# First operand from a channel-major copy of x; token-major x, its norm and the bias table later

## The chip, the cores and the metric

The kernel runs on one core of one Trainium2 chip. A core has TensorE (matmuls), VectorE, ScalarE, GpSimd and SyncE (which here only issues DMAs); the five run side by side, each takes its own instructions in order, and they wait for each other through semaphores. Sixteen DMA engines carry the loads of all queues. The metric is the device time of one execution in microseconds; the number that counts is the median of several.

## The reference, cut to what matters

Two transformer blocks run over 256 tokens of 2048 channels. All weights are read once, some 570 MB. The change is in the first step of the first block:

```
h    = x * rsqrt(mean(x*x) + eps) * g_mix_pre          # norm over the channels
proj = h @ w_in                                        # 2048 -> 5920
q, k, v ... = split(proj)                              # four kinds of attention, with bias tables
x    = x + rmsnorm(mix, g_mix_post)                    # x is needed again, token-major
```

The norm's factor is one number per token, so proj is (x * g_mix_pre) @ w_in, times that factor.

## The kernel before

**Operands.** A float32 product is made of three fp32r products: both operands are split into a top (rounded) and a rest, and top x top, rest x top and top x rest are summed in PSUM. ScalarE rounds a weight (`hi`, L769, writes w_hi), VectorE subtracts (`lo`, L1354, writes w_lo). The first operand lies with channels on partitions, in 16 chunks of 128 channels: HH (top) and HL (rest), tile h_hi_lo.

**Blocks and units.** The product goes block by block, 512 output columns each; blocks 0 to 11 are w_in. A block has 8 units, a unit two chunks of channels: 24 matmuls of 128 x 256 in block 0 (L2344; unit 0 of block 0 has lines of its own, L2329 and L2335). Weights come by SyncE's DMAs in tiles w_raw of 1 MB, four to a block, each for two units; a tile is loaded again once `lo` has read it (`weight_tile`, L471). ScalarE and VectorE run four units ahead of TensorE: in slot s they do the weights of unit s + 4 (`slot`, SPLIT_LEAD), each instruction in the order of the code.

**x at the start.** Only the token-major x is loaded, in pieces between the first weight tiles. `turn_first(j)` on TensorE transposes two chunks (four 128 x 128 transposes, L2519) into a PSUM bank, ScalarE multiplies by the gain and rounds (`round_gain`, L814), VectorE makes the rest (`rest_gain`, L1448). Pairs 0 and 1 are turned ahead of unit 0, pairs 2 and 3 after it, pair s + 3 after unit s. In slot s of ScalarE and VectorE the weights of unit s + 4 come first, and pair s + 3 behind them. A few matmuls of ones (`keep_busy`, L2510) run while the first data comes.

**The norm and the table.** ScalarE squares x in slots 5 and 6 and takes the root in slot 7; VectorE makes two diagonals (`rstd_diagonals`, L1489), TensorE turns them into a row (`rstd_row`, after unit 9), and VectorE scales block 0 out of PSUM in slot 10 (`project_out(0)`, L1505), which frees the bank for block 2 (unit 16). The factor on x itself is applied in slots 12 and 13 (L849). The bias table is a small matmul after unit 2 (`tables`, L2533), read out by VectorE in slot 3 (L1479).

**GpSimd's DMA queue.** It loads the table's inputs once tile 0 has landed, stores the table to DRAM when it is ready (L566), loads the first compression weight (L567, 2 MB, cmp_w); after block 0 is read out it loads the second (L577, 2 MB), and after block 1 it copies that block's output to the compression's input (L583 and L584, eight copies, cmp_x). VectorE adds a term to these (L1520, cmp_z) in slot 19, and TensorE runs 64 matmuls with cmp_z in slot 21 (L2547).

Of the kernel before, what the change touches and what calls it, by code (L numbers as in the profile page):

```python
# [201 lines left out]
def program(nc, a, out_n):  # L202
    ctx = ExitStack()
    with ctx:
# [51 lines left out]
        RROW = at("rstd_row", 71 * K, [P, T])  # L256
        X2 = [at(f"cmp_x2_{kv}", A0 + (65 - 6 * kv) * K, [P, 2, T]) for kv in range(2)]
# [173 lines left out]

        def soft(u, what):

            at0 = 12 * (u % 2) + 4 * ("max", "sum", "inv").index(what)
            return TINY[:, at0:at0 + 4]
# [26 lines left out]
        def _(sp):  # L462
# [51 lines left out]
            sp.dma_start(IDN[:, :], a["ident"]).then_inc(S("first_loaded"), 16)  # L514
            sp.dma_start(X[:, :, 0:T], x_tok[:, :, 0:T]).then_inc(S("first_loaded"), 16)
            for b in range(B_WOUT):
                for j in range(4):
                    src = rows(a["w_in"], j * 4 * P, P * CH_AT[b], P * block_chunks(b))
                    if b == 0 and j == 0:
                        sp.dma_start(RAW[:, 0, 0:2, :], src[:, 0:2, :]).then_inc(S("w_first"), 16)  # L520
                        sp.dma_start(X[:, :, T:2 * T], x_tok[:, :, T:2 * T]).then_inc(S("x_loaded0"), 16)
                        sp.dma_start(RAW[:, 0, 2:4, :], src[:, 2:4, :]).then_inc(S("w_loaded0"), 16)
                        continue
                    if b == 0:
                        sp.dma_start(cols512(X, j), cols512(x_tok, j)).then_inc(S(f"x_loaded{j}"), 16)
                    if b == 0 and j == 1:
                        sp.dma_start(PR[:, 16:NPRM], a["prm"][:, 16:NPRM]).then_inc(S("prm_loaded"), 16)
                    weight_tile(b, j, src)
# [20 lines left out]
        def _(pool):  # L549
# [11 lines left out]
            pool.wait_ge(S("w_loaded0"), 16)  # L561
# [189 lines left out]
        def _(act):  # L751
# [58 lines left out]
            def round_gain(n, j, gain):  # L810

                act.wait_ge(S("turned"), TURN0[n] + j + 1)
                for cc in range(2):
                    ins = act.activation(HH[:, 2 * j + cc, :], PB[j % 3][:, T * cc:T * cc + T], ACT.Identity,  # L814
                                         scale=prm(gain, 2 * j + cc))
                ins.then_inc(S("tok_hi"), 1)

            def round_mod(n, j, bank, u32, dst, gain, shift, col):

                act.wait_ge(S("turned"), TURN0[n] + j + 1)  # L820
# [16 lines left out]
            def x0_squares(half):  # L837

                for piece in range(2 * half, 2 * half + 2):
                    act.wait_ge(S(f"x_loaded{piece}"), 16)  # L840
# [54 lines left out]
            for s in range(SLOTS):  # L895
# [15 lines left out]
                if s < WIN_SLOTS:  # L911
# [4 lines left out]
                    if s == 3:  # L916
                        act.wait_ge(S("prm_loaded"), 16)
                        act.activation(TINY[:, 64:96], prm("c", 0, 32), ACT.Exp, scale=-1.0).then_inc(S("sigmoid_exp"), 1)
# [5 lines left out]
                    if s in (5, 6):  # L924
                        x0_squares(s - 5)
                    if s == 7:
                        root(0)
                    if s in (12, 13):
                        act.wait_ge(S("rstd"), 1)
                        scale_x0(s - 12, RST[:, 0, :])  # L930
# [410 lines left out]
        def _(dve):  # L1341
# [101 lines left out]
            def rest_gain(n, j, gain):  # L1443

                dve.wait_ge(S("tok_hi"), TURN0[n] + j + 1)
                for cc in range(2):
                    c = 2 * j + cc
                    ins = dve.scalar_tensor_tensor(HL[:, c, :], PB[j % 3][:, T * cc:T * cc + T], prm(gain, c),  # L1448
                                                   HH[:, c, :].bitcast(F32), ALU.mult, ALU.subtract)
# [18 lines left out]
            dve.wait_ge(S("first_loaded"), 48)  # L1468
# [203 lines left out]
            for s in range(SLOTS):  # L1672
# [31 lines left out]
                if s < WIN_SLOTS:  # L1704
# [578 lines left out]
        def _(pe):  # L2283
# [29 lines left out]
            def gemm_half(b, g, s, kk, top, rest, ready=None):  # L2313

                n = block_chunks(b) if g is None else 4
                if kk == 0:
# [4 lines left out]
                    if b == 0 and s == 0:  # L2321
                        pe.wait_ge(S("hi_ready"), 1)
                    else:
                        pe.wait_ge(S("lo_ready"), count(b, g, UPB, s + 1))
                k = 2 * s + kk
                if b == 0 and s == 0:
                    for m in range(n):
                        for i, x in enumerate((top, rest)):
                            pe.matmul(gview(0)[:, m, :], WH[:, 0, kk, P * m:P * m + P], x[:, k, :],  # L2329
                                      start=k == 0 and m % 2 == 0 and i == 0, stop=False, skip_group_check=True)  # L2330
                    if kk == 1:
                        pe.wait_ge(S("lo_ready"), 1)
                        for m in range(n):
                            for k in range(2):
                                ins = pe.matmul(gview(0)[:, m, :], WL[:, 0, k, P * m:P * m + P], top[:, k, :], start=False, stop=False,  # L2335
                                                skip_group_check=True)
                        ins.then_inc(S("unit_used"), 1)
                    return
# [173 lines left out]
            def turn_first(j):  # L2512

                bank(j % 3, "tok_lo", TURN0[0] + j + 1)
                if j > 0:
                    pe.wait_ge(S(f"x_loaded{j // 2}"), 16)
                for cc in range(2):
                    for tb in range(2):
                        ins = pe.transpose(PB[j % 3][:, T * cc + P * tb:T * cc + P * tb + P],  # L2519
                                           X[:, tb, T * j + P * cc:T * j + P * cc + P], IDN[:, :])  # L2520
                ins.then_inc(S("turned"), 1)
# [109 lines left out]
            for s in range(SLOTS):  # L2631
# [379 lines left out]
```

## Time and profile before

| | us |
|---|---|
| median of 3 runs | 2616.28 (2615.32 to 2616.51) |
| the profiled execution | 2615.8 |
| its span, first to last instruction | 2614.0 |
| TensorE busy | 2589.7 (99%) |
| VectorE busy | 1873.7 (72%) |
| ScalarE busy | 1379.0 (53%) |
| GpSimd busy | 351.5 (13%) |
| read from memory | 566.84 MB, 218 GB/s over the span |

Times of rows are microseconds from the span's start. PE is TensorE, PEld its weight load, DVE VectorE, ACT ScalarE, POOL GpSimd, SP SyncE. "Busy" of TensorE is modelled and does not mean that it is at its peak. The square bracket at the end of a row is the idle time of that engine ahead of the instruction and who ended it. A share of time over the whole span says little about the first 80 us; for these one reads the chain of waits and the instructions in order of time.

### The profile page before, as it was taken

How to read it: one execution, taken by the hardware profiler on the slowest of the kernel's cores; microseconds unless marked ns; L12 is line 12 of the kernel's file. 1: busy time of each engine (PE TensorE's matmuls, PEld its weight loads, DVE VectorE, ACT ScalarE, POOL GpSimd, SP SyncE). 2: the span in 40 equal slices, each digit the busy share in tenths (PEclk: the TensorE clock that was granted, in tenths of full speed). 3: DMA queues.
4: the chain of work that ended last, by engine and by line, in shares of the span. 5: the costliest groups of instructions: out<-in, count | busy, mean ns of one | idle time of the engine just before them, and what ended most of it. 6: DMA issues, size and time to landing. Idle time of an engine off the chain costs nothing.

```text
span 2614.0 us, 39368 instructions
## 1 busy us (share of the span) xinstructions
PE 2589.7 (99%) x16340; PEld 2292.6 (88%) x16340; DVE 1873.7 (72%) x2241; ACT 1379.0 (53%) x1877; POOL 351.5 (13%) x305
## 2 busy tenths in 40 slices
PE   9999999999999999999999999999999999999998
PEld 9888976998998888889999899998898888888887
DVE  5555666999999877787678967677656785446555
ACT  5455553554444554566874346666464454453454
POOL 0332321010000210200010311120011020020111
PEclk9999999999999999999999999999999999999999
DMA  9655554678687888877566745456667786655653
GB/s 319 181 167 162 158 169 149 230 252 305 244 292 274 290 314 292 298 268 218 162 216 243 273 129 153 146 149 218 208 199 250 252 295 215 189 188 193 192 192 129
DMA packets 287569, 573.19 MB, mean 219 GB/s; under 512 B 9886, under 2 KB 29105, under 8 KB 286880
## 3 DMA queue, kind: packets, MB, share of 16 engines
q1 hardware_dynamic: 281456, 548.69, 62.3%
q0 software_dynamic: 5936, 22.00, 2.9%
q8 instruction: 129, 2.11, 0.3%
q14 instruction: 48, 0.39, 0.0%
HBM read 566.84 MB, written 3.28 MB: 218 GB/s over the span
## 4 chain that ended last, share of the span: by engine, by line
PE 93%; DVE 4%; ACT 2%; issue 1%; POOL 0%; ACTq 0%; DVEq 0%; POOLq 0%
PE p_gemm L2410 31%; PE p_gemm L2344 30%; PE p_gemm L2307 13%; PE p_gemm L2309 7%; PE p_gemm L2370 3%; DVE w_lo L1354 1%; PE p_gemm L2423 1%; PE p_b L2596 1%; ACT w_hi L769 1%; PE p_b L2627 1%; PE p_b L2690 1%; PE p_b L2797 1%; PE p_b L2806 1%; PE p_b L2456 0%; PE p_gemm L2363 0%
## 5 line engine op out<-in xcount | busy, mean ns | idle before, releaser
L1354 DVE TENSOR_TENSOR w_lo<-w_raw,w_hi 128x1024 fp32r<-128x1024 f32 (+1 forms) x864 | 1070.6, 1244 | 621.9 <-ACT w_hi L769 620.1
L769 ACT ACTIVATE w_hi<-w_raw 128x1024 fp32r<-128x1024 f32 (+1 forms) x864 | 897.3, 1040 | 1096.4 <-PE p_gemm L2410 426.2
L2344 PE MATMUL p_gemm<-h_hi_lo,w_hi 128*128 128x256 f32 x2864 | 519.5, 284 | 0.6 <-DVE w_lo L1354 0.6
L2307 PE MATMUL p_gemm<-h_hi_lo,w_hi 128*128 128x512 f32 x1472 | 515.9, 395 | 0.0
L2344 PEld LDWEIGHTS p_gemm<-h_hi_lo,w_hi 128*128 128x128 f32 x2864 | 439.7, 189 | 8.4 <-issue 4.9
L2309 PE MATMUL p_gemm<-h_hi_lo,w_lo 128*128 128x256 f32 x1472 | 413.7, 281 | 0.0
L2344 PE MATMUL p_gemm<-h_hi_lo,w_lo 128*128 128x256 f32 x1432 | 402.6, 281 | 0.0
L2410 PE MATMUL p_gemm<-w_hi,a_hi 128*128 128x512 f32 x1008 | 393.4, 390 | 0.0
L2410 PE MATMUL p_gemm<-w_hi,a_lo 128*128 128x512 f32 x1008 | 392.7, 390 | 0.0
L2410 PE MATMUL p_gemm<-w_lo,a_hi 128*128 128x512 f32 x1008 | 392.6, 389 | 0.0
L2307 PEld LDWEIGHTS p_gemm<-h_hi_lo,w_hi 128*128 128x128 f32 x1472 | 276.4, 188 | 64.9
L1408 DVE SCALAR_TENSOR_TENSOR ada_w<-ada_w,silu_c 128x512 f32<-128x512 f32 x360 | 299.3, 831 | 8.3 <-DMA ada_w<-in_w_ada 7.8
L2344 PE MATMUL p_gemm<-l_hi,w_hi 128*128 128x256 f32 x1024 | 294.0, 287 | 0.0
L2344 PE MATMUL p_gemm<-l_lo,w_hi 128*128 128x256 f32 x1024 | 287.9, 281 | 0.0
L2344 PE MATMUL p_gemm<-l_hi,w_lo 128*128 128x256 f32 x1024 | 287.9, 281 | 0.0
L2309 PEld LDWEIGHTS p_gemm<-h_hi_lo,w_lo 128*128 128x128 f32 x1472 | 277.7, 189 | 0.5
L2344 PEld LDWEIGHTS p_gemm<-h_hi_lo,w_lo 128*128 128x128 f32 x1432 | 270.0, 189 | 0.0
L2410 PEld LDWEIGHTS p_gemm<-w_hi,a_hi 128*128 128x128 f32 x1008 | 189.3, 188 | 39.8
L2410 PEld LDWEIGHTS p_gemm<-w_hi,a_lo 128*128 128x128 f32 x1008 | 189.2, 188 | 39.5
L2410 PEld LDWEIGHTS p_gemm<-w_lo,a_hi 128*128 128x128 f32 x1008 | 189.3, 188 | 38.9
L2344 PEld LDWEIGHTS p_gemm<-l_hi,w_hi 128*128 128x128 f32 x1024 | 193.1, 189 | 3.7 <-issue 2.1
L2344 PEld LDWEIGHTS p_gemm<-l_lo,w_hi 128*128 128x128 f32 x1024 | 193.2, 189 | 1.1 <-issue 1.0
(440 smaller groups left out, 2864.9 us busy)
## 6 DMA issues: line engine op xcount, KB each, us to landing
w_raw<-in_w_mlp SPq DMA_DIRECT2D x128, 1024.0 KB, 5.7
w_raw<-in_w_in SPq DMA_DIRECT2D x107, 1024.0 KB, 5.7
ada_w<-in_w_ada SPq DMA_DIRECT2D x96, 1024.0 KB, 6.1
w_raw<-in_w_up SPq DMA_DIRECT2D x64, 1024.0 KB, 8.7
w_raw<-in_w_down SPq DMA_DIRECT2D x64, 1024.0 KB, 9.4
w_raw<-in_w_out SPq DMA_DIRECT2D x32, 1024.0 KB, 5.1
w_raw<-in_w_in SPq DMA_DIRECT2D x36, 768.0 KB, 4.9
cmp_w<-in_phi_w POOLq DMA_DIRECT2D x2, 2048.0 KB, 14.9
```

What stands on the lines that cost most here:

```text
L769: act.activation(WH[:, s % 4, :, 0:n], RAW[:, s // 2, 2 * (s % 2):2 * (s % 2) + 2, 0:n], ACT.Copy)\
L1354: dve.tensor_tensor(WL[:, s % 4, :, 0:n], RAW[:, s // 2, 2 * (s % 2):2 * (s % 2) + 2, 0:n], WH[:, s % 4, :, 0:n].bitcast(F32), ALU.subtrac ...
L1408: ins = dve.scalar_tensor_tensor(w, w, SIL[:, k, 0:1], before, ALU.mult, ALU.add)
L2307: pe.matmul(G[half][:, m, :], WH[:, s % 4, i, cols], HHL[:, k, :, :].rearrange("p z t -> p (z t)"), start=k == 0, stop=False, skip_group_c ...
L2309: ins = pe.matmul(G[half][:, m, T:2 * T], WL[:, s % 4, i, cols], HH[:, k, :], start=False, stop=k == KC - 1, skip_group_check=True)
L2344: ins = pe.matmul(dst, w[:, s % 4, kk, cols], x[:, k, :], start=k == 0 and m % 2 == 0 and i == 0, stop=k == KC - 1 and i == 2, skip_group_ ...
L2370: ins = pe.matmul(dst, x[:, k, toks], w[:, s % 4, kk, cols], start=first and i == 0 and (tb == 0 or b != V_HALF), stop=last and i == 2, sk ...
L2410: ins = pe.matmul(G[b % 2][:, tb, 0:n], x[:, k, toks], w[:, s % 4, kk, 0:n], start=k == 0 and i == 0, stop=k == KC - 1 and i == 2, skip_gr ...
L2423: ins = pe.matmul(G[b % 2][:, tb, :], x[:, k, P * tb:P * tb + P], w[:, s % 4, kk, :], start=False, stop=k == KC - 1 and i == 2, skip_group ...
L2596: ins = pe.matmul(ps[g][:, col:col + keys.shape[-1]], q[rows, P * z:P * z + P], keys[rows, :], start=True, stop=True)
L2627: ins = pe.matmul(ps[HD * g:HD * g + HD, queries], PJ[:, CH[vc], P * blk + HD * g:P * blk + HD * g + HD], PTS[:, g, probs], start=blk == 0 ...
L2690: ins = pe.matmul(ps[:, :], DF[:, i, dc, P * f:P * f + P], h[:, dc, :], start=dc == 0, stop=dc == 1)
```

## The change

A second array `xT` is passed in, x with channels on partitions. SyncE loads it in pieces of two and four chunks into a tile x_turned (at 64 KB, a place that is free then) where the pieces of x stood. ScalarE and VectorE make the tops and rests of the first operand straight from it; the transposes go. ScalarE loads its table by a dummy instruction ahead of the data. Token-major x is loaded behind block 0's last weight tile and ahead of block 1's first, and SyncE waits for each piece of x_turned before the piece of x that shares its semaphore. ident (64 KB) and the rest of prm (172 KB) are loaded after weight tile 2. The table's inputs (87 KB) are asked for when weight tile 2 has landed (before: tile 0). The squares go to slots 8 and 9, the root to 10, the diagonals to 10, rstd_row and project_out(0) from slots 9 and 10 to 12 and 13, the scaling of x to 14 and 15, the table's matmul from after unit 2 to after unit 5 and its reading to slot 6. Unit 0's 24 matmuls are put in the order top x top, rest, w_lo. The warming matmuls are 11 in one group, before 8 and 3.

```diff
-            sp.dma_start(IDN[:, :], a["ident"]).then_inc(S("first_loaded"), 16)
-            sp.dma_start(X[:, :, 0:T], x_tok[:, :, 0:T]).then_inc(S("first_loaded"), 16)
+            sp.dma_start(XT[:, 0:2, :], a["xT"][:, 0:2, :]).then_inc(S("first_loaded"), 16)
...
-                        sp.dma_start(X[:, :, T:2 * T], x_tok[:, :, T:2 * T]).then_inc(S("x_loaded0"), 16)
+                        x_turned(0, 2, 4)
...
                     if b == 0:
+                        x_turned(j, 4 * j, 4 * j + 4)
+                    weight_tile(b, j, src)
+                    if b == 0 and j == 2:
+                        sp.dma_start(PR[:, 16:NPRM], a["prm"][:, 16:NPRM]).then_inc(S("prm_loaded"), 16)
+                        sp.dma_start(IDN[:, :], a["ident"]).then_inc(S("prm_loaded"), 16)
+                if b == 0:
+                    for j in range(4):
+                        sp.wait_ge(S(f"x_loaded{j}"), 16)
                         sp.dma_start(cols512(X, j), cols512(x_tok, j)).then_inc(S(f"x_loaded{j}"), 16)
...
-            pool.wait_ge(S("w_loaded0"), 16)
+            pool.wait_ge(S("w_loaded2"), 16)
...
-                act.wait_ge(S("turned"), TURN0[n] + j + 1)
+                if n == 0:
+                    x_arrived(act, j)
+                else:
+                    act.wait_ge(S("turned"), TURN0[n] - TURN0[2] + j + 1)
                 for cc in range(2):
-                    ins = act.activation(HH[:, 2 * j + cc, :], PB[j % 3][:, T * cc:T * cc + T], ACT.Identity,
+                    ins = act.activation(HH[:, 2 * j + cc, :], gain_src(n, j, cc), ACT.Identity,
                                          scale=prm(gain, 2 * j + cc))
...
-            act.wait_ge(S("first_loaded"), 48)
+            act.wait_ge(S("ones_ready"), 1)
+            act.activation(TINY[:, 61:62], ONE[:, 0:1], ACT.Identity)
...
-                    if s in (5, 6):
-                        x0_squares(s - 5)
-                    if s == 7:
+                    if s in (8, 9):
+                        x0_squares(s - 8)
+                    if s == 10:
                         root(0)
-                    if s in (12, 13):
+                    if s in (14, 15):
...
-                    if s == 3:
+                    if s == 6:
                         tables()
-                    if s == 7:
+                    if s == 10:
                         rstd_diagonals()
-                    if s == 10:
+                    if s == 13:
                         rstd_row()
                         project_out(0)
...
-            keep_busy(1, 8)
-            pe.wait_ge(S("first_loaded"), 48)
-            turn_first(0)
-            keep_busy(2, 3)
-            turn_first(1)
+            keep_busy(1, 11)
...
-                if s == 0:
-                    turn_first(2)
-                if s + 3 < 8:
-                    turn_first(s + 3)
-                if s == 2:
+                if s == 5:
                     tables()
-                if s == 9:
+                if s == 12:
                     rstd_row()
```

## Rows read from the trace of the kernel before

**Rows 1.** The page: busy time and share of the span of each engine.

```profile
PE 2589.7 (99%) x16340; PEld 2292.6 (88%) x16340; DVE 1873.7 (72%) x2241; ACT 1379.0 (53%) x1877; POOL 351.5 (13%) x305
```

**Rows 2.** Chain of waits to 80 us: start, duration, engine, tile, line, count.

```profile
10.78 2.13 PE p_gemm L2329 x16
...
21.29 0.75 PE p_b L2533 x2
...
22.05 3.11 PE p_gemm L2344 x24
25.15 0.43 PE p_b L2519 x4
...
28.87 14.20 PE p_gemm L2344 x120
...
60.54 15.39 PE p_gemm L2370 x66
75.94 0.74 issue
76.67 7.10 PE p_b L2547 x64
```

**Rows 3.** Instructions in order of time, TensorE's weight loads: start, duration, instruction.

```profile
22.05 0.30 PEld L2344 LDWEIGHTS p_gemm<-h_hi_lo,w_hi 128*128 128x128 f32 x2 [0.71 <-DVE h_hi_lo L1448]
```

**Rows 4.** Instructions in order of time, ScalarE.

```profile
7.56 1.28 ACT L814 ACT_TABLE_LOAD   x1 [7.56 <-PE p_b L2519]
...
18.89 1.06 ACT L769 ACTIVATE w_hi<-w_raw 128x1024 fp32r<-128x1024 f32 x1 [1.82 <-DMA w_raw<-in_w_in]
19.85 0.82 ACT L814 ACTIVATE h_hi_lo<-p_b,prm 128x256 fp32r<-128x256 f32 x2
...
22.91 1.06 ACT L769 ACTIVATE w_hi<-w_raw 128x1024 fp32r<-128x1024 f32 x1 [0.56 <-DMA w_raw<-in_w_in]
...
28.53 1.06 ACT L769 ACTIVATE w_hi<-w_raw 128x1024 fp32r<-128x1024 f32 x1 [1.38 <-PE p_gemm L2344]
```

**Rows 5.** Instructions in order of time, VectorE.

```profile
19.98 1.23 DVE L1354 TENSOR_TENSOR w_lo<-w_raw,w_hi 128x1024 fp32r<-128x1024 f32 x1 [1.46 <-ACT w_hi L769]
21.12 0.87 DVE L1448 SCALAR_TENSOR_TENSOR h_hi_lo<-p_b,prm,h_hi_lo 128x256 fp32r<-128x256 f32 x2
...
41.09 0.48 DVE L1489 TENSOR_SCALAR gain_row<-ident,ss_rstd 128x128 f32<-128x128 f32 x2
...
49.13 1.23 DVE L1505 TENSOR_TENSOR proj<-p_gemm,rstd_row 128x1024 f32<-128x1024 f32 x1
...
74.57 2.00 DVE L1520 TENSOR_TENSOR cmp_z<-cmp_x,prm 128x240 f32<-128x240 f32 x4
```

**Rows 6.** Two stretches: length, engines' busy us, granted clock, DMA share, GB/s.

```profile
8.00:16.00 8.00, 6.43 (x53) 6.09 (x52) 4.81 (x8) 5.97 (x10) 1.76 (x3) 1.00 1.03 362
16.00:24.00 8.00, 7.99 (x64) 7.12 (x63) 6.37 (x9) 5.62 (x10) 0.00 (x0) 1.00 1.05 387
```

**Rows 7.** SyncE's issue of block 1's first tile, and its DMA line (us to landing).

```profile
13.84 0.37 SPq L471 DMA_DIRECT2D w_raw<-in_w_in  x1
...
w_raw<-in_w_in SPq DMA_DIRECT2D x1, 1024.0 KB, 11.8
```

**Rows 8.** GpSimd's issues, then DMA lines of compression weights and last input copy.

```profile
50.65 1.16 POOL L577 DMA_DIRECT2D cmp_w<-in_phi_w  x1 [19.66 <-DVE proj L1505]
64.39 0.55 POOL L583 DMA_DIRECT2D cmp_x<-proj  x1 [12.57 <-DVE proj L1505]
...
68.04 0.52 POOL L584 DMA_DIRECT2D cmp_x<-proj  x1
...
cmp_w<-in_phi_w POOLq DMA_DIRECT2D x1, 2048.0 KB, 16.9
...
cmp_w<-in_phi_w POOLq DMA_DIRECT2D x1, 2048.0 KB, 12.9
...
cmp_x<-proj POOLq DMA_DIRECT2D x1, 63.8 KB, 3.7
```

More of the change, by code:

```diff
@@ L256, in program @@
         RROW = at("rstd_row", 71 * K, [P, T])
+        XT = at("x_turned", 64 * K, [P, KC, T])
         X2 = [at(f"cmp_x2_{kv}", A0 + (65 - 6 * kv) * K, [P, 2, T]) for kv in range(2)]
@@ L430, in pair_banks, with gain_src, x_arrived @@
             return PBS[:, 2 * (u % 2):2 * (u % 2) + 2, :]
+        def gain_src(n, j, cc):
+            return XT[:, 2 * j + cc, :] if n == 0 else PB[j % 3][:, T * cc:T * cc + T]
+        def x_arrived(engine, j):
+            if j == 0:
+                engine.wait_ge(S("first_loaded"), 32)
+            else:
+                engine.wait_ge(S(f"x_loaded{j // 2}"), 16)
         def soft(u, what):
@@ L513, in _, with x_turned @@
             sp.dma_start(prm("g_mix_pre", 0, 16), a["prm"][:, 0:16]).then_inc(S("first_loaded"), 16)
-            sp.dma_start(IDN[:, :], a["ident"]).then_inc(S("first_loaded"), 16)
-            sp.dma_start(X[:, :, 0:T], x_tok[:, :, 0:T]).then_inc(S("first_loaded"), 16)
+            sp.dma_start(XT[:, 0:2, :], a["xT"][:, 0:2, :]).then_inc(S("first_loaded"), 16)
+            def x_turned(j, c0, c1):
+                sp.dma_start(XT[:, c0:c1, :], a["xT"][:, c0:c1, :]).then_inc(S(f"x_loaded{j}"), 16)
             for b in range(B_WOUT):
@@ L839, in x0_squares @@
                 for piece in range(2 * half, 2 * half + 2):
-                    act.wait_ge(S(f"x_loaded{piece}"), 16)
+                    act.wait_ge(S(f"x_loaded{piece}"), 32)
                 for tb in range(2):
@@ L1447, in rest_gain @@
                     c = 2 * j + cc
-                    ins = dve.scalar_tensor_tensor(HL[:, c, :], PB[j % 3][:, T * cc:T * cc + T], prm(gain, c),
+                    ins = dve.scalar_tensor_tensor(HL[:, c, :], gain_src(n, j, cc), prm(gain, c),
                                                    HH[:, c, :].bitcast(F32), ALU.mult, ALU.subtract)
@@ L2315, in gemm_half @@
                 n = block_chunks(b) if g is None else 4
+                if b == 0 and s == 0:
+                    if kk == 0:
+                        pe.wait_ge(S("tok_hi"), 1)
+                        pe.wait_ge(S("hi_ready"), 1)
+                        for k in range(2):
+                            for m in range(n):
+                                pe.matmul(gview(0)[:, m, :], WH[:, 0, k, P * m:P * m + P], top[:, k, :],
+                                          start=k == 0 and m % 2 == 0, stop=False, skip_group_check=True)
+                        return
+                    pe.wait_ge(S("tok_lo"), 1)
+                    for k in range(2):
+                        for m in range(n):
+                            pe.matmul(gview(0)[:, m, :], WH[:, 0, k, P * m:P * m + P], rest[:, k, :], start=False, stop=False,
+                                      skip_group_check=True)
+                    pe.wait_ge(S("lo_ready"), 1)
+                    for k in range(2):
+                        for m in range(n):
+                            ins = pe.matmul(gview(0)[:, m, :], WL[:, 0, k, P * m:P * m + P], top[:, k, :], start=False, stop=False,
+                                            skip_group_check=True)
+                    ins.then_inc(S("unit_used"), 1)
+                    return
                 if kk == 0:
@@ L2320, in gemm_half @@
                         pe.wait_ge(*gemm_free(b))
[L2321 to L2324, printed above, removed]
+                    pe.wait_ge(S("lo_ready"), count(b, g, UPB, s + 1))
                 k = 2 * s + kk
[L2326 to L2338, printed above, removed]
                 for m in range(n):
```

22 lines of the change are left out of this document (5 added, 17 removed).

## The prediction

> **What bounds the kernel now.** I first read the page's busy line: TensorE is busy 2589.7 us of a span of 2614.0 [rows 1], so only TensorE time or TensorE waits count. Everything the diff touches is in the first 76 us, so I then read the chain of waits there [rows 2]: from 10.78 us it is TensorE almost without a break. A unit of block 0 (two 128-row chunks of weights, 24 matmuls) costs 2.84 us: five of them take 14.20. Four transposes cost 0.43. Block 0 runs as unit 0 at 10.78, unit 3 at 22.05 and units 5 to 9 from 28.87, so block 1 (unit 8) starts at 28.87 + 3 x 2.84 = 37.39. This is the mark against which I sum.
>
> Unit 3 is the one place after the start where TensorE waits: 0.71 us, for VectorE's rest of the first operand, and the two table matmuls at 21.29 (0.75 us) lie in the same hole [rows 2, 3]. ScalarE shows why: rounding the weights of unit 4 waits 1.82 us for a DMA and starts at 18.89; only behind it comes the gain of chunk pair 3 at 19.85; VectorE then does the weights' rest (19.98) and the operand's rest (21.12, 0.87 us) [rows 4, 5]. From the landing of weight tile 2 at about 18.85 to unit 3 at 22.05 is 3.2 us. So the start is bounded by DMA, through the in-order queues of ScalarE and VectorE, and the transposes are partly covered by it. The same happens with tile 3 (18.89 becomes 22.91, wait 0.56) [rows 4]. The DMA engines move 387 GB/s there at a share of 1.05 [rows 6]: they are full. The first tile of block 1 is issued at 13.84 and takes 11.8 us, so it lands at 25.6; its rounding starts at 28.53 and waits for TensorE, not for DMA: 2.9 us of slack [rows 4, 7].
>
> **The change part by part.**
>
> *Transposes out.* 32 transposes go, eight groups of 0.43 = 3.5 us of TensorE, six of them between unit 0 and unit 5 [rows 2]. At the start the table load (1.28 us at 7.56, behind a wait for the transposes [rows 4]) goes ahead of the data, so unit 0 comes sooner, by at most the two of them, 1.28 + 0.87 = 2.2 us: 8.6, done at about 11.6. None of this is a gain by itself; what is late next decides. The warming matmuls stay 11 in number.
>
> *Unit 3.* Bytes ahead of tile 2 in SyncE's queue: 236 KB fewer (the rest of prm, 172, and ident, 64, go behind it), and the tables' 87 KB are asked for after it: 0.33 MB at 387 GB/s = 0.85 us [rows 6]. Tile 2 lands at 18.0. With the same chain behind it (round 4, gain 3, both rests: 3.2 us) unit 3 starts at 21.2 instead of 22.05. TensorE is ready long before: even with unit 0 at the old 10.78, three units end at 10.78 + 8.8 = 19.6. So of everything saved ahead of unit 3, 0.85 us arrive; the rest becomes idle time.
>
> *Units 3 to 6.* Unit 3 after a wait takes 3.11 [rows 2]: to 24.3. Units 4 and 5 without transposes: 30.0. The tables' matmuls stand here now, no longer in a hole: + 0.75 = 30.75. Unit 6 ends at 33.6. In the kernel before, it ended at 34.55, so the gain here is 0.95.
>
> *The reload.* Token-major x is 2 MB more, queued ahead of block 1's first tile. The bytes up to tile 3 are the same, and it lands at 22.85. Behind it are 3 x 1024 KB = 3.15 MB; at 387 GB/s 8.1 us [rows 6]: the tile of block 1 lands at 30.95 instead of 25.6. The last piece of x_turned lies 1 MB ahead of tile 3's end, 22.85 - 2.7 = 20.1; SyncE's new waits end there, before the queue drains, so they cost nothing of their own, but the four token-major loads and every later weight tile stand behind them. ScalarE's rounding of unit 8 wanted to start when unit 4 is done (27.1); it waits 3.8 us, and behind it on ScalarE is the gain of chunk pair 7, and behind that VectorE's rest, for which unit 7 waits. The chain is again 3.2 us: unit 7 starts at 34.15, 0.55 after TensorE is ready, takes 3.11 and unit 8 starts at 37.25. Against 37.39 that is -0.15 us. So nearly all of the 3.5 + 2 us is spent waiting for the same DMA engines. Bounds: with the reload costing no wait, unit 8 at 36.45 (-0.95); with DMA at the 362 GB/s of 8 to 16 us [rows 6], landing 8.7 after 22.85, +0.4. I take the 387, the row of this stretch. Later tiles land each 2.7 us apart against 5.7 us of use and catch up.
>
> The Trainium skill (DMA: Bandwidth & Descriptors, section on the anatomy of one DMA) gives about 2.0 us plus bytes over 436 GB/s for a DMA. By that rate the 3.15 MB would take 7.2 us, the tile would not bind unit 7, and the sum would be -0.95. The trace disagrees with it: 387 with all engines busy.
>
> *Norm and table three units later.* The squares, root and diagonal (ready at 41.56 [rows 5]) move by 8.5 us with ScalarE two squares behind: about 50, needed at the end of unit 12, 51.3. project_out(0) (49.13 to 50.35 [rows 5]) moves to 57.6 to 58.9; it frees the bank that block 2 takes at 60.54 [rows 2]. Both are covered, by 1.3 and 1.6 us; a lag beyond that is paid one for one. Scaling x two units later has no near reader. Cost 0, bound +1.
>
> *GpSimd's queue.* It now waits for tile 2, then for the table (ready after slot 6 instead of 3, 8.5 us later), stores it and loads the first compression weight; the second (50.65 us before) waits for project_out(0): about 59.1. It took 12.9 us to land [rows 8], so it lands at 72.0 instead of 63.6. Behind it in the same queue are the eight copies of the compression input, issued 64.39 to 68.04, the last landing in 3.7 us, at 71.7 [rows 8]. They now follow the weight: 72 at the soonest, 72.0 + 3.7 = 75.7 at the latest. The reader is VectorE's add at 74.57, and TensorE stands idle 0.74 us for its end at 76.57 [rows 2, 5]. So this is a second critical place with 2.8 us of slack before and 0 to 2.6 after: cost 0 to 1.1 us. I take 0, since 0.5 MB at 387 GB/s is 1.4 us, landing 73.4.
>
> **Sum.** -0.15 + 0 + 0 = about -0.1. The profiled execution took 2615.8 (span 2614.0 and 1.8 around it); 2615.7 for the new one. The median is 0.5 above it: 2616.2.
>
> **The rivals.**
>
> *A, slower: the compression input comes late.* The mechanism is the one above: the copies queue behind a 2 MB load that starts 8.5 us later. It hurts from 74.57 on, and by over 0.2% (5.2 us) from 79.8 on. If the second weight takes as long as the first (16.9 [rows 8]), it lands at 76.0, and if the copies then need their whole old stretch (64.39 to 71.7, 7.3 us), at 83.3: 8.7 us late, 2624.9. Against it: 16.9 was with the table's store ahead of it, and the copies are issued by then and need only to move. The mild form, +1.1, gives 2617.3.
> The Trainium skill (DMA: Bandwidth & Descriptors, "Queues, rings and completion order") says that descriptors of one ring are consumed in order. By that rule the copies can't pass the weight; no row of before shows the case.
>
> *B: the clock falls in the new holes.* From unit 0's end at 11.6 and two units more (17.3) to 21.2 TensorE stands idle 3.9 us, in one hole or, by where tile 1 lands, two. If it went from 2.4 to 1.2 GHz, a unit would cost 2.84 more, of which 0.55 is slack ahead of unit 7: 2618.5. Against it: between 8 and 16 us TensorE was busy 6.43 of 8.00, so 1.57 us of idle stood before unit 0 too, at a granted clock of 1.00, and its first 16 matmuls took 2.13, 0.133 each against 0.118 [rows 2, 6].
> The Trainium skill (TensorE: Matmul & The Clock Gate, Part 1) lets an idle TensorE fall to half rate; the trace shows no fall after the 1.57.
>
> *C: the reload binds nothing,* because landings spread differently than I draw them: 2615.3; and if tile 2 also came sooner, each us of that counts, at most 37.39 - 32.2 (unit 0 done at 11.6, seven units, the tables) = 5.2: 2611. For it: the small offsets. Against it: engines at a share of 1.05.
>
> **How the numbers follow.** Forecast (2615.4 to 2616.9) 0.70; A mild 0.09, A over 5.2 us 0.04; B 0.05; C 0.12, of it 0.01 beyond 0.2%. The range takes the forecast, A mild and most of C: 2614.4 to 2618.0. Faster or slower by over 0.2% is about what a measurement of this kernel can tell from no change. Faster 0.01, same 0.95, slower 0.04.
>
> **What would show it.** The profile after should have no L2519 transposes; ScalarE waiting for w_raw by DMA before rounding units 2, 4 and 6 and, longest (3 to 4 us), unit 8; TensorE idle some 4 us in all before unit 3 and 0.5 before unit 7; the tables' matmuls after unit 5; unit 8 at 37.2; GpSimd's second compression load at 59; and TensorE's wait ahead of its 64 compression matmuls at 0.7 to 1.8 us. I am wrong if unit 8's tile lands before 30 (C), if that last wait is over 2 (A), or if the granted clock is below 1.00 in the first 40 us (B).

## The result and the profile after

| | before | changed |
|---|---|---|
| median, 18 runs each | 2616.17 us (2615.13 to 2616.75) | 2620.95 us (2617.49 to 2622.96) |
| ratio, 95% interval | | 1.0017 (1.0011 to 1.0024) |
| the profiled execution | 2615.8 us | 2619.44 us |
| its span | 2614.0 us | 2617.6 us |

One of the 18 executions of the changed kernel took 8356.39 us for a reason that is not known; the range above leaves it out, and without it the median is 2620.90.

The change makes the kernel 4.8 us slower, outside the predicted range, and its time varies more from run to run (5.5 us against 1.6). The transposes are gone, and TensorE is busy 1.3 us less than in [rows 1]. First the page's busy line, then the chain of waits (start, duration, what), which answers [rows 2]:

```profile
PE 2588.4 (99%) x16308; PEld 2289.2 (87%) x16308; DVE 1874.6 (72%) x2241; ACT 1380.0 (53%) x1878; POOL 351.9 (13%) x305
```

```profile
19.51 11.25 DMA w_raw<-in_w_in
...
30.78 1.07 ACT w_hi L790
31.88 1.23 DVE w_lo L1379
33.10 0.80 DVE h_hi_lo L1473 x2
...
33.95 17.31 PE p_gemm L2373 x144
51.26 0.43 PE p_b L2552 x2
51.69 5.69 PE p_gemm L2373 x48
...
67.90 8.84 DMA cmp_x<-proj
76.76 1.95 DVE cmp_z L1544 x4
...
78.84 8.61 PE p_b L2561 x64
```

The chain is no longer TensorE's. It runs through block 1's first weight tile (L1379 and L790 were L1354 and L769), and from 57.4 us through ScalarE and VectorE to the copies of the compression input and to cmp_z, until 78.84; before, TensorE's 64 compression matmuls began at 76.67 [rows 2]. They also take 8.61 us instead of 7.10.

Three rows of the instructions in order of time, TensorE: start, duration, and in the brackets the idle time ahead of it.

```profile
20.32 0.50 PE L2373 MATMUL p_gemm<-h_hi_lo,w_hi 128*128 128x256 f32 x2 [1.62 <-DVE h_hi_lo L1473]
33.95 0.51 PE L2373 MATMUL p_gemm<-h_hi_lo,w_hi 128*128 128x256 f32 x2 [1.07 <-DVE h_hi_lo L1473]
...
78.84 8.61 PE L2561 MATMUL p_b<-cmp_w,cmp_z 128*30 128x256 f32 x64 [3.23 <-DVE cmp_z L1544]
```

TensorE ends its earlier work at 78.84 - 3.23 = 75.61, 0.33 sooner than before (75.94 [rows 2]): the front part gained a third of a microsecond. Then it stands idle 3.23 us instead of 0.74. The busy times by stretch (length, TensorE, its weight load, VectorE, ScalarE, GpSimd, granted clock, DMA share, GB/s) show what the idle time did to the clock:

```profile
76.00:78.00 2.00, 0.00 (x0) 0.00 (x0) 1.24 (x3) 0.00 (x0) 0.00 (x0) 1.00 1.03 246
78.00:79.00 1.00, 0.15 (x2) 0.19 (x4) 0.97 (x3) 0.00 (x0) 0.01 (x1) 0.76 1.05 258
79.00:80.00 1.00, 1.00 (x6) 0.45 (x5) 0.94 (x3) 0.00 (x0) 1.00 (x2) 0.50 1.05 258
80.00:81.00 1.00, 1.00 (x8) 0.47 (x6) 1.00 (x1) 0.00 (x0) 0.42 (x1) 0.50 1.02 238
81.00:82.00 1.00, 1.00 (x8) 0.57 (x6) 1.00 (x2) 0.00 (x0) 0.00 (x0) 0.53 1.04 227
82.00:83.00 1.00, 1.00 (x14) 0.55 (x11) 0.25 (x1) 0.00 (x0) 0.00 (x0) 1.00 1.02 227
```

The granted clock falls to 0.50 (1.2 of 2.4 GHz) in the hole and stays there to nearly 82 us: 8 matmul passes in a microsecond instead of 14. The sum: the compression begins 78.84 - 76.67 = 2.17 us later and takes 8.61 - 7.10 = 1.51 longer, 3.7; the spans differ by 3.6.

Why cmp_z is late, in the rows that answer [rows 8]: GpSimd's issues, then lines of the DMA issues in short windows (size, us to landing): the second compression weight, the copies issued about 64.2, the last copy, issued at 67.90, and SyncE's weight tile issued about 63.

```profile
58.83 1.16 POOL L598 DMA_DIRECT2D cmp_w<-in_phi_w  x1 [19.20 <-DVE proj L1529]
64.24 0.55 POOL L604 DMA_DIRECT2D cmp_x<-proj  x1 [4.24 <-DVE proj L1529]
...
67.90 0.52 POOL L605 DMA_DIRECT2D cmp_x<-proj  x1
...
cmp_w<-in_phi_w POOLq DMA_DIRECT2D x1, 2048.0 KB, 13.7
...
cmp_x<-proj POOLq DMA_DIRECT2D x1, 64.0 KB, 6.7
...
cmp_x<-proj POOLq DMA_DIRECT2D x1, 63.8 KB, 8.8
...
w_raw<-in_w_in SPq DMA_DIRECT2D x1, 1024.0 KB, 15.4
```

The second weight goes 8.2 us later and lands at 72.5; the last copy lands at 67.90 + 8.8 = 76.7 instead of 71.7, though it is issued no later. The first copy lands at 70.9, 1.6 us ahead of the weight in front of it in the same queue, so the copies don't simply wait for the weight to land. And the weight tile issued at 63 takes 15.4 us, where the tile of that time took 7.2 before.

Whose bytes move beside the copies is in the lines of the DMA queues (q0 is GpSimd's, q1 SyncE's; packets, MB, share of the 16 engines). Before, from 64 to 66 and from 68 to 70 us:

```profile
q1 hardware_dynamic: 300, 0.58, 96.8%
...
q0 software_dynamic: 170, 0.33, 68.8%
q1 hardware_dynamic: 43, 0.08, 23.5%
```

Changed, the same two stretches:

```profile
q0 software_dynamic: 171, 0.70, 103.0%
q1 hardware_dynamic: 3, 0.00, 0.7%
...
q0 software_dynamic: 115, 0.38, 59.7%
q1 hardware_dynamic: 135, 0.28, 45.9%
```

In the changed kernel the second weight takes the engines while the copies are being asked for, and SyncE's tile, pushed back by it, then takes nearly half of them while the copies move.

### The profile page after: what moved, and what is told of

The parts are those of the page before. It is cut to its first block, busy times and chain, and to the rows that moved or that the text cites. A ratio compares the mean times of both kernels' runs of the same rounds, so it can differ in the third digit from the quotient of the medians.

```text
span 2617.6 us, 39301 instructions
## 1 busy us (share of the span) xinstructions
PE 2588.4 (99%) x16308; PEld 2289.2 (87%) x16308; DVE 1874.6 (72%) x2241; ACT 1380.0 (53%) x1878; POOL 351.9 (13%) x305
## 4 chain that ended last, share of the span: by engine, by line
PE 91%; DVE 4%; ACT 2%; DMA 1%; issue 1%; POOL 0%; SPq 0%; ACTq 0%; DVEq 0%
PE p_gemm L2439 31%; PE p_gemm L2373 29%; PE p_gemm L2331 13%; PE p_gemm L2333 7%; PE p_gemm L2399 3%; DVE w_lo L1379 2%; ACT w_hi L790 1%; DMA w_raw<-in_w_in 1%; PE p_gemm L2452 1%; PE p_b L2610 1%; PE p_b L2641 1%; PE p_b L2700 1%; PE p_b L2807 1%; PE p_b L2816 1%; PE p_b L2485 0%
## 5 line engine op out<-in xcount | busy, mean ns | idle before, releaser
L1379 DVE TENSOR_TENSOR w_lo<-w_raw,w_hi 128x1024 fp32r<-128x1024 f32 (+1 forms) x864 | 1070.2, 1243 | 629.1 <-ACT w_hi L790 627.8
L790 ACT ACTIVATE w_hi<-w_raw 128x1024 fp32r<-128x1024 f32 (+1 forms) x864 | 897.1, 1040 | 1103.9 <-PE p_gemm L2439 426.4
```

The source lines that it names most:

```text
L790: act.activation(WH[:, s % 4, :, 0:n], RAW[:, s // 2, 2 * (s % 2):2 * (s % 2) + 2, 0:n], ACT.Copy)\
L1379: dve.tensor_tensor(WL[:, s % 4, :, 0:n], RAW[:, s // 2, 2 * (s % 2):2 * (s % 2) + 2, 0:n], WH[:, s % 4, :, 0:n].bitcast(F32), ALU.subtrac ...
```

## The experiments

Two theories stand against each other. **Q**: the copies are late because they stand in GpSimd's queue behind a second weight that is asked for later. **C**: all sixteen DMA engines are full from 60 to 77 us, by the 2 MB more, by the loads of the table and the compression moved later, and by SyncE's tiles, and everything in that stretch lands late. Full engines alone don't tell the two kernels apart: their share is 0.95 to 1.05 from 60 to 76 us in the kernel before as well, and only from 76 to 80 is it 0.68 there against 1.04. What has to be told apart is whose bytes stand in the way. All ratios are against runs of the kernel before on the same chip, whose medians lie between 2616.04 and 2616.30 us; a difference from the 2620.95 of the changed kernel carries an error of some tenths more. Most runs are medians of 11 executions, w1_act_queue of 5, gain_first of 6.

**Run norm_back.** In the changed kernel:

```diff
-                    if s in (8, 9):
-                        x0_squares(s - 8)
-                    if s == 10:
+                    if s in (5, 6):
+                        x0_squares(s - 5)
+                    if s == 7:
                         root(0)
```

and likewise the diagonals (10 to 7), the row (12 to 9), project_out(0) (13 to 10), the scaling (14, 15 to 12, 13).

> The changed kernel with the norm's steps (squares, root, diagonals, row, reading of block 0) back in their old slots, everything else as changed. Theory Q (the loss comes from the second compression weight being asked for 8 us later, which makes the eight input copies and cmp_z late): the second weight is issued when the first has landed, at about 55 instead of 58.8, lands at 68 to 69, the copies land at 72 to 74, TensorE's wait ahead of its 64 compression matmuls is 0.7 to 1 us instead of 3.2, no fall of the clock, 2615.5 to 2616.5. Rival F (the loss is in the first 40 us, in the waits for DMA and the reload): the time stays at 2620 to 2621.

Measured: 2618.93 us, 1.0012 (1.0003 to 1.0021). The second weight goes at 56.35, bound by the first one's landing, and is through at about 67, before the last copies are issued. Still the copies take long (the line of cmp_x: DMA to landing, least, median, most):

```profile
DMA to landing us min/median/max: 6.2/6.9/8.0
```

2.0 of the 4.8 us go, less than Q expected (2615.5 to 2616.5). The last copy, issued at 67.66 with the weight already landed, takes 8.0 us instead of 3.7 [rows 8]; the first ones were still asked for behind it. TensorE waits 2.2 us and the 64 matmuls take 8.79.

**Run norm_late.** The kernel before with the same six places moved the other way.

> The kernel before with only the norm's steps three slots later (two for the scaling of x). Theory Q: the second compression weight is issued at 58.5 instead of 50.65, the copies land at 76 to 77, TensorE waits 3 us for cmp_z and the clock falls there: 2619 to 2621. Rival F: no change, 2616.2. Rival T (it needs the late table too, which delays the first compression weight): about 2616 to 2617.

Measured: 2617.25 us, 1.0005 (0.9996 to 1.0014), not told from no change and less than Q said. In the profiled execution cmp_z starts at 76.31, with a wait for the copies, TensorE waits 2.0 us and the 64 matmuls take 8.73 us. That execution took 2618.69 us; nine of the 11 took 2616.46 to 2617.51, so its trace shows one of the two worst, not a typical one.

**Run table_late.** The kernel before with

```diff
-            pool.wait_ge(S("w_loaded0"), 16)
+            pool.wait_ge(S("w_loaded2"), 16)
...
-                    if s == 3:
+                    if s == 6:
                         tables()
...
-                if s == 2:
+                if s == 5:
                     tables()
```

> The kernel before with only the table three units later: its inputs asked for after weight tile 2, the matmul after unit 5, its reading in slot 6. That makes the table's store and the first compression weight (2 MB) 8 us later, at about 38; the second weight can go only when the first has landed, at about 55 instead of 50.65. Theory C (not the queue but the fullness of all DMA engines between 60 and 77 us makes the input copies late; every load moved into or towards that stretch counts): copies land 6 to 8 us after their issue, cmp_z 0.5 to 1.5 late, 2617 to 2618. Rival N (only the norm's move matters): 2616.2.

Measured: 2617.16 us, 1.0008 (0.9999 to 1.0017). The second weight goes at 55.6, cmp_z at 75.60 after a wait of 0.73 for the copies. Two of the 11 executions took 2621.04 and 2621.72 us, the other nine 2618.20 or less.

**Run dup_load.** The kernel before with the extra traffic alone:

```diff
+                if b == 0:
+                    for j in range(4):
+                        n = 512 if j < 3 else 256
+                        sp.wait_ge(S(f"x_loaded{j}"), 16)
+                        sp.dma_start(DUP[:, :, 512 * j:512 * j + n], x_tok[:, :, 512 * j:512 * j + n]).then_inc(S(f"x_loaded{j}"), 16)
```

> The kernel before with 1.75 MB of token-major x loaded once more, where the changed kernel has its reload (behind block 0's last weight tile), into memory that nobody reads; the waits of SyncE ahead of it are there too. Block 1's first tile lands at about 30.4 instead of 25.6, its gain chain would bind unit 7 at 33.6, before TensorE is ready (34.55): no wait there. Theory C: the 4.6 us of extra traffic is absorbed in the slack of the DMA engines between 40 and 60 us: 2616.2, at most 2617. Rival R (the reload by itself is the loss): 2619 or more.

Measured: 2616.27 us, 1.0001 (0.9993 to 1.001). So none of the three parts is the loss by itself: +1.1, +1.1 and +0.2 us of medians against the kernel before on the same chip, none of them clear of no change, together 2.4 where the whole change costs 4.8 and saves in front. Each shows the same sign in its trace, though: cmp_z at 76.31, 75.60 and 76.24 instead of 74.57 [rows 5], each after a wait for the copies, and TensorE waits 2.0, 1.5 and 1.6 us instead of 0.74. (0.2 to 0.8 us of the later starts are only that TensorE comes to the compression that much later in these executions.)

**Run w1_act_queue.** In the changed kernel the second weight leaves GpSimd's queue:

```diff
-            pool.wait_ge(S("w1c_loaded"), 16)
-            pool.dma_start(W1C[1][:, :, :], ...).then_inc(S("w1c_loaded"), 16)
...
+                    if s == 14:
+                        act.wait_ge(*gemm_read(0))
+                        act.dma_start(W1C[1][:, :, :], ...).then_inc(S("first_loaded"), 16)
```

TensorE's wait for the weight moves to the other semaphore with it.

> The changed kernel with the second compression weight loaded by ScalarE's DMA queue in slot 14, at about the same time (58.6 to 59) as GpSimd loads it now. If the copies are late because they stand in GpSimd's queue behind 2 MB: they land 3.5 us after their issue again (71.5), TensorE waits 0.7 us or as long as the weight itself needs (it lands at 72 to 73), 2616 to 2617. If they are late because the DMA engines as a whole are full at that time: they land at 75 to 77 as now, 2620.

Measured: 2626.64 us, 1.004 (1.0028 to 1.0053). The weight lands 26.4 us after its issue. From its chain of waits:

```profile
58.73 26.45 DMA cmp_w<-in_phi_w
85.27 8.48 PE p_b L2563 x64
```

and the copies, now with nothing of that size ahead of them in their queue, land after 5.4 to 7.9 us. The last one, issued at 69.0, lands by 76.9. That is what the second half of its expectation says of the copies: they are as late without the weight in their own queue. The time is worse than either theory said, because the weight itself is late. The same bytes go in smaller packets from ScalarE's queue, q10 (from 62 to 64 us; below it GpSimd's queue in the changed kernel):

```profile
q10 hardware_dynamic: 418, 0.43, 62.6%
```

```profile
q0 software_dynamic: 112, 0.46, 62.0%
```

That is some 1.0 KB a packet against 4.1, and from 70 us on q10 moves 0.07 MB in two microseconds while each of the other two moves 0.16 to 0.33. That the packets' size is the reason is not shown.

**Run w1_early.** norm_back without GpSimd's wait for the first weight ahead of the second (one line out).

> norm_back (changed kernel, norm's steps in their old slots) and GpSimd doesn't wait for the first compression weight to land before it asks for the second: issued at about 51 instead of 56.4, both in line. Theory C: the 2 MB are through by 63 to 65, the copies land in 3.5 to 5 us, TensorE's wait is 0.7 to 1.2 us, no fall of the clock, 2615.7 to 2616.7 against 2618.9 of norm_back. If the DMA engines stay full to 77 us whatever is moved: 2618 to 2619.

Measured: 2621.15 us, 1.002 (1.0011 to 1.0028). The wrong way. The chain of waits shows who paid:

```profile
41.43 20.38 DMA w_raw<-in_w_in
```

With two compression weights side by side a weight tile landed after 20.4 us; block 1 was then read out late, the copies were issued 2.7 us later than in norm_back, and TensorE waited 4.3 us for cmp_z. The 64 matmuls took 9.33 us. Asking sooner for one load made another late.

**Run tiles_held.** The test of what SyncE's traffic does. In the changed kernel SyncE's tile of 63 us, and with it all that stands behind it in its queue, waits for the copies:

```diff
                     sp.wait_ge(S("lo_ready"), count(b - 1, None, UPB, 2 * j + 2))
+                    if b == 3 and j == 1:
+                        sp.wait_ge(S("x2_loaded"), 128)
```

> The changed kernel, but SyncE asks for the second tile of block 3 (issued at about 63) only when the eight input copies have landed; its reader needs it after 85. Theory C (the copies are late because the DMA engines are full with everybody's traffic): the second compression weight lands at about 70 to 71, the copies land at 72 to 74.5, TensorE's wait is 0.7 to 1.5 us instead of 3.2, the clock stays, 2616.5 to 2618. Rival Q2 (only the place behind the compression weight in GpSimd's queue matters, not SyncE's traffic): 2620 to 2621.

Measured: 2616.56 us, 1.0004 (0.9995 to 1.0013): 4.4 of the 4.8 us are back. GpSimd's last copy, the line of cmp_x (DMA to landing) and TensorE's waits from 40 to 100 us:

```profile
68.35 0.52 POOL L607 DMA_DIRECT2D cmp_x<-proj  x1
...
DMA to landing us min/median/max: 4.8/5.2/5.8
...
PE p_b L2563 <- DVE cmp_z L1546: 0.7, 1, 0.7
```

The second weight is asked for at 59.30, even later than in the changed kernel, and in the same queue; only SyncE's traffic is gone from beside it. It lands after 12.4 us instead of 13.7, the last copy by 74.2, and the wait is that of before. So Q2 is out: what the change loses needs SyncE's traffic beside the copies. Two of the 11 executions still took 2619.73 and 2619.83 us; no trace of them was read. And the copies are not back at 3.2 to 4.2 us: held, GpSimd's queue alone takes the engines from 68 to 70 us,

```profile
q0 software_dynamic: 188, 0.57, 106.5%
```

by what is left of the weight, the copies, and the four loads of 256 KB for att_bias that GpSimd asks for right behind them (at 68.9; in the kernel before too, at 68.55). No run moves those four.

**Run before_held.** The same two lines in the kernel before.

> The kernel before with the second tile of block 3 asked for only when the eight input copies have landed. There the copies land at 71.7, 2.8 us ahead of their reader, and the wait of 0.74 us ahead of the compression is VectorE's own order. Theory C: 2615.8 to 2616.4, no change. If holding the tile is a gain of its own: 2615.3 or less.

Measured: 2615.98 us, 0.9999 (0.999 to 1.0008). The copies land in 1.8 to 2.7 us instead of 3.2 to 4.2, and nothing comes of it: there the wait was VectorE's own order. Side by side, the slowest of the eight copies, from issue to landing:

| | second weight landed before the copies are asked for (kernel before) | asked for 8 us later (changed kernel) |
|---|---|---|
| SyncE's tile of 63 us asked for as usual | 4.2 us | 8.8 us |
| held (before_held, tiles_held) | 2.7 us | 5.8 us |

Both loads count, the tile for 1.5 and 3.0 us, the change for 3.1 and 4.6 (the columns differ in more than the weight). Holding the tile was enough, since the reader has slack for 5.8 us and not for 8.8.

**Run warm_hole.** Matmuls of ones in the changed kernel's hole:

```diff
             def compress():
 
+                keep_busy(CMP_BANKS[0], 8)
                 pe.wait_ge(S("w1c_loaded"), 32)
```

> The changed kernel with 8 matmuls of ones (0.24 us for each of 16 passes, 3.9 us) on TensorE ahead of its wait for cmp_z, so that it isn't idle there. If the hole costs the wait (about 2.5 us more than before) and a fall of the clock (8.61 against 7.10 us for the 64 matmuls, 1.5 us): the 64 matmuls take 7.1 again and the time falls by about 1 to 1.5, to 2619.5. If the clock has no part in it: unchanged or up to 0.7 slower, since the filling outlasts the wait.

Measured: 2618.94 us, 1.001 (1.0002 to 1.0019), 2.0 us less than the changed kernel. The 64 matmuls, busy time in one stretch, here and in the changed kernel:

```profile
76.00:86.00 10.00, 6.95 (x64) 3.58 (x64) 1.00 1.00 277
```

```profile
78.00:88.00 10.00, 8.61 (x64) 4.56 (x64) 0.83 0.84 235
```

Started at 79.1 they take 7.0 us at a granted clock of 1.00. In the traces they end 1.3 us sooner (86.15 against 87.45). So the hole costs twice: the wait, and the fallen clock behind it.

How long the hole is doesn't settle by itself whether the clock falls. It fell after holes of 2.0 (norm_late), 2.2 (norm_back), 3.2 (changed), 4.3 (w1_early) and 9.9 us (gain_first), and not after 1.5 (table_late), 1.6 (dup_load) and, further on, 2.1 (best1). Two almost equal holes, norm_back and then best1, from 78 to 79 us (granted clock 0.57 and 1.00):

```profile
78.00:79.00 1.00, 1.00 (x8) 0.56 (x6) 0.93 (x3) 0.00 (x0) 1.00 (x2) 0.57 1.08 256
```

```profile
78.00:79.00 1.00, 1.00 (x13) 0.62 (x10) 1.00 (x2) 0.00 (x0) 1.00 (x2) 1.00 1.08 195
```

**Run cmm_later.** The changed kernel with S_CMM = 22 instead of 21.

> The changed kernel with the 64 compression matmuls (and the small transposes behind them) after slot 22's first half instead of slot 21's, 2.8 us of other TensorE work later; all DMAs as in the changed kernel. If the whole loss is TensorE's idle time and the fall of the clock at this one place: wait 0 to 0.5 us, 64 matmuls in 7.1, and since the 0.74 us of before go too, 2615.5 to 2617. If the loss sits elsewhere: 2620 to 2621.

Measured: 2619.9 us, 1.0015 (1.0006 to 1.0024). The wait for cmp_z falls to 0.6 us and the clock stays, as expected; but the first attention unit needs gates that come out of the same slot. From TensorE's waits, 100 to 200 us:

```profile
PE p_b L2624 <- POOL att_e L645: 2.4, 1, 2.4
```

The place was right, but the cure moved too much along, and the time that was expected (2615.5 to 2617) didn't come.

**Run compress_shift.** The compression one slot later, the gates in their slots (ScalarE's exponent of the gates ahead of that of the gelu).

> The changed kernel with the whole compression (VectorE's adds, the 64 matmuls, the gelu and what follows) one slot later, while the gates and their transposes, which the first attention unit needs, stay in their slots. All DMAs as in the changed kernel. If the loss is TensorE's idle time at this place: wait under 1 us, 64 matmuls in 7.1 us, no new wait at the first probabilities, and the front's 0.5 us and part of the 0.74 us of before are seen: 2615 to 2616.5. If late DMAs hurt elsewhere too: 2618 or more.

Measured: 2616.7 us, 1.0004 (0.9995 to 1.0013). The copies are as late as in the changed kernel (up to 8.9 us), TensorE waits 0.2 us for cmp_z and 0.4 at the first probabilities. So late DMAs hurt at this place, and elsewhere by no more than the 0.6 us that are left against the kernel before. The median is 0.2 above what was expected.

**Run gain_first.** In the changed kernel, on ScalarE and VectorE alike:

```diff
-                    slot(b, None, s % UPB)
                     if s + 3 < 8:
                         round_gain(0, s + 3, "g_mix_pre")
+                    slot(b, None, s % UPB)
```

> The changed kernel with one exchange in the slots of ScalarE and VectorE: the gain and rest of chunk pair s + 3 ahead of the weights of unit s + 4. The prediction's chain (weight tile lands, rounding, gain, both rests, 3.2 us) should then not hold units 3 and 7: unit 3 starts at about 18.5 instead of 20.3, unit 7 is not held by block 1's first tile; unit 8 is, at 33.2 instead of 36.8. The gain of 3 to 3.5 us in front then meets the late copies: TensorE comes to the compression 3 us sooner and waits there as much longer. Theory C: 2619 to 2621, no better than the changed kernel. If the front's gain lasts: 2617 to 2618.

Measured: 2623.27 us, 1.0028 (1.0017 to 1.004), 2.3 slower than the changed kernel, and 2.3 over the end of the expectation. The front works: the hole ahead of unit 3 is gone, and unit 8 starts at 33.96, after a wait of 0.25 us and some 3 us sooner. But GpSimd's copies follow TensorE's slots and come 2.8 us sooner, while the second weight goes 1.1 us later (59.97), when the first has landed. So the copies stand 1.4 us behind it in the same queue, where it was 5.4, and take 11.8 to 15.5 us; the weight lands at 76.1. Here the weight ahead of the copies and SyncE's tiles act together, and the run can't tell them apart. From the chain of waits, and TensorE's waits from 40 to 100 us:

```profile
38.44 20.96 DMA cmp_w<-in_phi_w
...
65.05 15.53 DMA cmp_x<-proj
```

```profile
PE p_b L2561 <- DVE cmp_z L1544: 9.9, 1, 9.9
```

The last copy, issued at 65.05, lands at 80.6, later than that issued at 67.90 in the changed kernel (76.7).

**Run best1.** gain_first, compress_shift, and token-major x piece by piece behind block 1's weight tiles.

> gain_first and compress_shift together, and token-major x loaded piece by piece behind block 1's weight tiles instead of ahead of them. The front: unit 3 at 18.5, block 1's first tile lands at 25 to 26, unit 8 starts at about 32.5 to 33.5. The compression's copies bind by the DMA engines at 74 to 76; TensorE reaches the compression at about 74.5 (one unit later than before, 3.5 sooner by the front): wait of 1 to 4 us. 2612.5 to 2615.5, below both kernels. If the DMA engines' fullness takes all of it: 2616 or more.

Measured: 2615.65 us, 0.9998 (0.9989 to 1.0007). The median is 0.15 over the end of the expectation. TensorE waits 2.1 us for cmp_z; no change that can be told.

**Runs best2 and best3.** best1 with SyncE's tile held as in tiles_held; best3 holds from `b == 3 and j == 0`.

> best1 (gains first, token-major x behind block 1's tiles, compression one slot later) with the second tile of block 3 held until the copies have landed. In best1 the copies land at 75.6 and TensorE waits 2.1 us for them. Theory C: they land at 72 to 73.5, the wait falls to 0.2 to 0.8, 2613.5 to 2614.5. Rival (the compression weights themselves fill the engines): 2615.6 as best1.

> As best2, but held from the first tile of block 3 on (asked for at about 53 in best1). The second compression weight lands 2 to 3 us sooner, the copies at 70 to 72; but three tiles then come late, and the rounding of block 3 may wait for them. Theory C: 2613 to 2614 if the tiles still come in time, 2616 or more if block 3's first unit waits for its weights.

Measured: best2 2613.41 us, 0.9989 (0.998 to 0.9998); best3 2612.65 us, 0.9986 (0.9977 to 0.9995). In best2 TensorE still waits 1.2 us, more than was said, for copies that land by 74.5. In best3, where they land by 69, there is no wait of TensorE from 40 to 100 us, and the time is 0.35 under the expectation. Its chain of waits from 27 us, the line of cmp_x, and ScalarE's wait for the held tile:

```profile
27.62 20.07 PE p_gemm L2377 x168
47.69 0.43 PE p_b L2556 x2
48.12 8.52 PE p_gemm L2377 x72
56.64 15.40 PE p_gemm L2403 x66
...
75.34 7.08 PE p_b L2565 x64
```

```profile
DMA to landing us min/median/max: 2.5/3.0/3.8
...
76.39 1.06 ACT L791 ACTIVATE w_hi<-w_raw 128x1024 fp32r<-128x1024 f32 x1 [5.88 <-DMA w_raw<-in_w_in]
```

The tile comes late enough for ScalarE to wait 5.9 us, and TensorE, at its 64 matmuls meanwhile, doesn't feel it. This version beats both kernels, by 3.6 us against the one before. Neither half has done it alone: the front and the later compression without the hold are best1, a hold without them is before_held, and both are no change.

## Why the prediction was wrong

**The front was right.** Unit 3 was put at 21.2 and starts at 20.32, because tile 2 landed at 17.13 and not at 18.0, and TensorE's idle time before it was put at about 4 us and is 2.6 (0.94 and 1.62); neither mattered, since unit 7 waited for block 1's tile, 1.07 us where 0.55 was said; block 1's first tile was put at 30.95, and the rounding behind it starts at 30.78; unit 7 was put at 34.15 and starts at 33.95; the gain at the start of the compression was put at 0.15 and is 0.33. Nearly all of the time of the 32 transposes is spent waiting for DMA, as the sum had it, and the clock stays at 1.00 in the first 40 us. The norm's steps and project_out(0) were covered, as the sum had it.

**The step that failed is the term of GpSimd's queue, "cost 0 to 1.1 us. I take 0".** It named the right place and chain, and mis-sized the landing: it put the last copy at 72 to 75.7 us and took 73.4, from 0.5 MB at the full rate and from the 3.7 us of one copy of before as the upper end. It landed at 76.7. The weight was priced nearly right (72.0, and it landed at 72.5). But the copies didn't have the engines to themselves behind it: from 68 to 70 us GpSimd's queue had 0.60 of them and moved 0.38 MB, and SyncE's tile had 0.46. Neither price allowed for that tile: the 3.7 us were measured when a tile landed in 7.2 us, and the prediction itself had the engines fuller than before. "Later tiles ... catch up" was said of the tiles, which had 20 us of lead, and not asked of the copies, which had 2.8. tiles_held gives the size: 4.4 us come back when SyncE's queue is held from that tile on, the slow clock's part among them.

**The second failure is rival B, put in the wrong place.** The fall of the clock was priced for the holes ahead of units 2 and 3 (0.94 and 1.62 us in the trace, no fall) and never for the one place where the prediction itself let a wait grow. The hole of 3.23 us there brought a fall and 1.5 us more; warm_hole took 2.0 us of median back, 1.3 in the traces. A mild form of rival A priced at 1.1 us is one of 2.2 + 1.5 once both are in.

The Trainium skill (TensorE: Matmul & The Clock Gate, Part 1) has an idle TensorE fall to half its clock; the trace agrees for the 3.23 us and shows none for 1.62.

**Rival A's mechanism was right in part.** It had the copies late because the second weight starts 8.5 us later ahead of them in one queue. That they share a queue isn't needed: with the weight in ScalarE's queue (w1_act_queue), and with the weight landed before the last copy was asked for (norm_back), they still took up to 8 us. Nor is it so that "the copies can't pass the weight": the first one landed 1.6 us ahead of it. But the later weight does count, with tiles_held at 5.8 us against before_held at 2.7, and in gain_first, where it stood 1.4 us ahead of them, up to 15.5. The Trainium skill (DMA: Bandwidth & Descriptors, "Issuing engines are not separate DMA queues") says that all issuing engines share the same DMA engines and interleave there; tiles_held agrees, 8.8 us down to 5.8 for the slowest copy by holding SyncE's tile alone.

**What stays open.** The single profiled execution loses 3.6 us, the median 4.8; that the slower executions lose more at the same place is likely by tiles_held, but no trace of one of them was read. The parts added one by one to the kernel before give 2.4 of 4.8 us, none clear of no change; that they grow together through the wait's effect on the clock fits norm_late's trace (8.73 us for the matmuls) and table_late's (7.10, a shorter hole), but the split of the loss among reload, norm and table was not settled. What the loads for att_bias behind the copies cost them was not tried, nor why the load from ScalarE's queue took 26.4 us, nor why the clock fell after one hole of 2.2 us and not after one of 2.1.

## What to carry to other kernels

Where work is taken off the busiest engine at the price of traffic, ask of each small, late-issued transfer with a waiting reader what lands beside it, not only what it waits behind; its latency measured beside other traffic is no upper bound. A prefetch with 20 us of lead can be held for it at no cost to TensorE: that gave the changed kernel 4.4 us back, and it was the hold and the shorter front together that beat the kernel before by 3.6 (best3); by itself the hold gave it nothing. And price a wait that grows on TensorE with the slow clock behind it: here it came with holes from 2.0 us on, though not with each of them.

## What was not expected of the hardware

A 2 MB load of the same data at the same time landed after 13.7 us from GpSimd's queue and after 26.4 from ScalarE's, beside SyncE's tiles; its packets were 1.0 KB instead of 4.1. Copies of 64 KB took 1.8 to 2.7 us (before_held), 3.2 to 4.2 (before), up to 8.8 (changed) and up to 15.5 us (gain_first), by what moved beside and ahead of them. And a copy asked for sooner can land later: the last copy of gain_first, issued at 65.05, landed at 80.6, that of the changed kernel, issued at 67.90, at 76.7.
